# Who reads with a stride: rows written in plain order by VectorE, and transposes on TensorE that read every 8th or 4th column

## What is computed

```python
def rms_norm(x, g):
    y = x * lax.rsqrt(jnp.mean(x * x, axis=-1, keepdims=True) + EPS)
    return y * g
...
    # every token takes 2 of 32 experts; tokens are sorted by expert into blocks of 128
    def expert_block(args):
        xblk, e = args                       # 128 tokens x 1024
        hid = jax.nn.silu(xblk @ w_gate[e]) * (xblk @ w_up[e])     # 128 x 512
        return hid @ w_down[e]               # 128 x 1024
...
    x = x + hierarchical_moe(rms_norm(x, norm_ffn_g), ...)
```

## Time and profile before

| | |
|---|---|
| median of 3 runs | 2146.08 us (2141.89 to 2154.14) |
| the profiled execution | 2152.06 us, span of its trace 2150.2 us |
| TensorE busy | 2092.8 us, 97% |
| VectorE busy | 1303.7 us, 61% |
| ScalarE busy | 1073.8 us, 50% |
| mean DMA rate | 184 GB/s, up to 395 GB/s in the slices of the expert stage |

### The profile page before, as it was taken

The page is one execution under the profiler, slowest core; times in us unless marked ns, Lnnn a source line. Parts: engine busy times, 40 slices in busy tenths (PEclk is TensorE's granted clock), DMA queues, the critical chain, the costliest instruction groups (busy, mean ns, idle before and its releaser), DMA issues.

```text
span 2150.2 us, 30216 instructions
## 1 busy us (share of the span) xinstructions
PE 2092.8 (97%) x10268; PEld 1730.2 (80%) x10268; DVE 1303.7 (61%) x1645; ACT 1073.8 (50%) x1582; POOL 511.6 (24%) x653
## 2 busy tenths in 40 slices
PE   8999999999999999999999999989999999999997
PEld 7788888888788888897888888757788788878886
DVE  5654233465555233555643434458899999899994
ACT  4453333343442332344523232137787788778884
POOL 4251011220541011213500012113212234332221
PEclk9999999999999999999999999999999999999999
DMA  7213222433213323452122225579999998997973
GB/s 229 92 40 98 88 87 92 173 130 108 74 40 108 98 79 98 163 171 69 40 85 82 81 96 205 206 271 357 386 395 394 394 340 299 392 384 262 325 260 88
DMA packets 108657, 396.72 MB, mean 184 GB/s; under 512 B 9282, under 2 KB 15603, under 8 KB 82964
## 3 DMA queue, kind: packets, MB, share of 16 engines
q1 hardware_dynamic: 91812, 335.64, 42.0%
q0 software_dynamic: 16752, 59.83, 10.5%
HBM read 402.78 MB, written 34.60 MB: 203 GB/s over the span
## 4 chain that ended last, share of the span: by engine, by line
PE 42%; DMA 10%; DVE 2%; issue 2%; ACT 2%; SPq 0%; POOL 0%; POOLq 0%; ACTq 0%; DVEq 0%
DMA held_wu<-w_up_e 5%; PE main L512 3%; PE main L514 3%; PE main L513 3%; DMA y<-e_yo,e_prv 2%; PE main L500 2%; PE main L502 2%; PE main L501 2%; PE main L1988 2%; PE main L1990 2%; PE main L1989 2%; DMA e_xg<-h2s,e_nxt 2%; PE main L1976 2%; PE main L1975 2%; PE main L1974 2%
## 5 line engine op out<-in xcount | busy, mean ns | idle before, releaser
L959 DVE TENSOR_TENSOR w_lo<-raw,w_hi 128x1024 fp32r<-128x1024 f32 (+1 forms) x216 | 250.3, 1180 | 320.3 <-ACT w_hi L705 320.2
L705 ACT ACTIVATE w_hi<-raw 128x1024 fp32r<-128x1024 f32 (+1 forms) x216 | 211.7, 1006 | 141.9 <-PE main L514 73.9
L512 PE MATMUL main<-e_g_hi,w_hi 128*128 128x512 f32 x576 | 237.6, 413 | 0.0
L514 PE MATMUL main<-e_g_hi,w_lo 128*128 128x512 f32 x576 | 226.1, 392 | 0.0
L513 PE MATMUL main<-e_g_lo,w_hi 128*128 128x512 f32 x576 | 225.4, 391 | 0.0
L500 PE MATMUL main<-w_hi,e_g_hi 128*128 128x512 f32 (+1 forms) x560 | 203.6, 364 | 2.3 <-DVE e_g_lo L973 2.3
L502 PE MATMUL main<-w_hi,e_g_lo 128*128 128x512 f32 (+1 forms) x560 | 200.2, 357 | 0.0
L501 PE MATMUL main<-w_lo,e_g_hi 128*128 128x512 f32 (+1 forms) x560 | 200.0, 357 | 0.0
L2097 DVE TENSOR_TENSOR e_d_lo<-held_wd,e_d_hi 128x2048 fp32r<-128x2048 f32 x76 | 173.1, 2288 | 36.2 <-ACT e_d_hi L2034 36.1
L2097 DVE TENSOR_TENSOR e_u_lo<-held_wu,e_u_hi 128x2048 fp32r<-128x2048 f32 x76 | 173.7, 2285 | 25.6 <-ACT e_u_hi L2034 25.6
L2097 DVE TENSOR_TENSOR e_g_lo<-held_wg,e_g_hi 128x2048 fp32r<-128x2048 f32 x76 | 173.5, 2283 | 2.5 <-ACT e_g_hi L2034 2.4
(11 more groups left out here) (349 smaller groups left out, 4786.5 us busy)
## 6 DMA issues: line engine op xcount, KB each, us to landing
held_wg<-w_gate_e SPq DMA_DIRECT2D x78, 1024.0 KB
held_wu<-w_up_e SPq DMA_DIRECT2D x78, 1024.0 KB
held_wd<-w_down_e SPq DMA_DIRECT2D x76, 1024.0 KB
raw<-w_in SPq DMA_DIRECT2D x120, 512.0 KB, 3.6
raw<-w_proj_b SPq DMA_DIRECT2D x24, 512.0 KB, 3.6
raw<-w_proj_a SPq DMA_DIRECT2D x24, 512.0 KB, 3.6
raw<-w_out SPq DMA_DIRECT2D x24, 512.0 KB, 4.2
raw<-w_in SPq DMA_DIRECT2D x24, 256.0 KB, 4.6
```

What stands on the lines that cost most here:

```text
L512: pe.matmul(bank[:], hi[:, k, :], mov_hi[:, k, :], start=(k == 0), stop=False)
L514: mm = pe.matmul(bank[:], lo[:, k, :], mov_hi[:, k, :], start=False, stop=(k == KT - 1))
L705: act.activation(hi, buf, ACT.Copy).then_inc(w_hi_done, 1)
L959: dve.tensor_tensor(lo, buf, hi.bitcast(F32), ALU.subtract).then_inc(w_split, 1)
```

## The change

A helper `every(rows, n, k)` gives the view of every n-th column from column k on. VectorE's two instructions (three places in the code) lose their rearranged views and read and write in plain order. All transposes of `h2`, `xg` and `hid` take `every(...)` where they took 128 adjacent columns. `h2s` thus holds rows in natural order, and the turned tiles `h2T`, `xT` and `hidT` hold exactly what they held. The instructions, their number, their engines and their order are the same in both kernels.

```diff
+def every(rows, n, k):
+
+    return rows.rearrange("p (q k) -> p k q", k=n)[:, k, :]
...
                 for k in range(4):
-                    c = (4 * b + k) * P
-                    mm = pe.transpose(bank[:, k * P:(k + 1) * P], rows[:, c:c + P], ident)
+                    mm = pe.transpose(bank[:, k * P:(k + 1) * P], every(rows, KT, 4 * b + k), ident)
...
-            dve.scalar_tensor_tensor(out=rows.rearrange("p (k q) -> p k q", q=P),
-                                     in0=x2[:, t, :].rearrange("p (q k) -> p k q", q=P),
-                                     scalar=rsf[:, t:t + 1],
-                                     in1=gf_row.rearrange("p (q k) -> p k q", q=P),
-                                     op0=ALU.mult, op1=ALU.mult).then_inc(h2_ready, 1)
+            dve.scalar_tensor_tensor(out=rows, in0=x2[:, t, :], scalar=rsf[:, t:t + 1], in1=gf_row, op0=ALU.mult, op1=ALU.mult).then_inc(h2_ready, 1)
...
                 for k in range(4):
-                    c = (4 * b + k) * P
-                    mm = pe.transpose(ps_x[b][:, k * P:(k + 1) * P], xg[:, c:c + P], ident)
+                    mm = pe.transpose(ps_x[b][:, k * P:(k + 1) * P], every(xg, KT, 4 * b + k), ident)
...
             for k in range(DE // P):
-                mm = pe.transpose(ps_h[:, k * P:(k + 1) * P], hid[:, k * P:(k + 1) * P], ident)
+                mm = pe.transpose(ps_h[:, k * P:(k + 1) * P], every(hid, DE // P, k), ident)
...
-            dve.scalar_tensor_tensor(out=hid.rearrange("p (k q) -> p k q", q=P),
-                                     in0=th.rearrange("p (q k) -> p k q", q=P), scalar=0.5,
-                                     in1=ps_u[:].rearrange("p (q k) -> p k q", q=P),
-                                     op0=ALU.mult, op1=ALU.mult).then_inc(hid_done, 1)
+            dve.scalar_tensor_tensor(out=hid, in0=th, scalar=0.5, in1=ps_u[:], op0=ALU.mult, op1=ALU.mult).then_inc(hid_done, 1)
```

More of the change, by code:

```diff
@@ L1630, in turn_x @@
             for k in range(4):
-                c = (4 * b + k) * P
-                mm = pe.transpose(bank[:, k * P:(k + 1) * P], xg[:, c:c + P], ident)
+                mm = pe.transpose(bank[:, k * P:(k + 1) * P], every(xg, KT, 4 * b + k), ident)
             mm.then_inc(s_x_ps, 1)
@@ L1660, in turn_hidden @@
         for k in range(DE // P):
-            mm = pe.transpose(bank[:, k * P:(k + 1) * P], hid[:, k * P:(k + 1) * P], ident)
+            mm = pe.transpose(bank[:, k * P:(k + 1) * P], every(hid, DE // P, k), ident)
         mm.then_inc(s_h_ps, 1)
@@ L1712, in glu @@
             dve.wait_ge(s_h_ps, s)
-        dve.scalar_tensor_tensor(out=hid.rearrange("p (k q) -> p k q", q=P), in0=th[s].rearrange("p (q k) -> p k q", q=P), scalar=0.5,
-                                 in1=main[2 * s + 1][:].rearrange("p (q k) -> p k q", q=P), op0=ALU.mult,
-                                 op1=ALU.mult).then_inc(s_hid_done, 1)
+        dve.scalar_tensor_tensor(out=hid, in0=th[s], scalar=0.5, in1=main[2 * s + 1][:], op0=ALU.mult, op1=ALU.mult).then_inc(s_hid_done, 1)
     held["chosen_dve"] = {"glu": glu}
```

## The result

The changed kernel takes 2139.24 us (median of 14 runs, 2135.10 to 2143.47); beside it, on the same chip, the kernel before took 2149.48 us (14 runs, 2141.69 to 2161.65). The ratio is 0.9949 [0.9933, 0.9966]: about 11 us or 0.5% faster. Predicted was 2185.2, 1.8% slower. The sign was wrong.

A forecast was written before the change was run, and what follows sets the result against it. The prediction took TensorE, 97% busy, as the bound, with DMA-bound stretches among the expert blocks. Its slower transposes added 41.1 us, less VectorE's 2.0: +39.1 on the median 2146.08 gave 2185.2 us, 1.8% slower, range 2140 to 2212.

The forecast's parts named there:

- the pricing of TensorE's load: TensorE's stepped transposes: each exposed load costs 0.113 us more eight apart, 0.100 four apart, taken from VectorE's rows; 1.09 a block.
- if it gets longer, the row gets longer by as much: TensorE's rows of transposes: the load is exposed, so extra load time lengthens the row, except for a row's first load.
- the 41.1 us of the sum: TensorE's added transpose time over expert blocks, last block, chosen blocks and turns of h, before subtracting VectorE's 2.0 us.
- The reading that the load is what spaces the transposes: TensorE's transposes: 0.109 us apart where the identity's stream would need 0.057, so the weight load sets the spacing.
- The first rival: TensorE's load does not care how its columns lie; only 2.0 us gained, 2144, no measurable change; chance 19%.
- the four places on the chain: Chain of waits: VectorE's rewritten instructions count only at h_last and three times at e_hid, 2.0 us gained.
- one long wait for a gather: Expert intervals from 1833.00 to 1928.40 us: the wait absorbs TensorE's extra time, adding between 0 and 5.4, taken as +1.5.
- h_last (0.8 forecast): Rewritten VectorE instruction on the chain of waits, there at 2.09 us: the cheaper norm gains 0.8 us.
- The second rival: Expert blocks: the shorter glu starts weight loads earlier, shrinking TensorE's 19.7 us of waiting; 2124 at best; chance 3%.
- the loop of weight loads: DMA-bound expert blocks: chain circles through weight load (13.88), ScalarE's rounding (1.93) and VectorE's remainder (2.30).
- The third: TensorE's stepped load takes three times the plain one (+0.218 us); about 2236 us; chance 5%.
- VectorE's own prices: VectorE's plain instructions: norm_f 2181 to 1280 ns, glu's second half 1079 to 680 ns; 26.8 us less work.

The follow-up runs named there:

- t9: Kernel before, with the turn of xg done four times over in each expert block (32 transposes, 128 adjacent columns each): 2228.95 us, one run.
- t10: Changed kernel, with the turn of xg done four times over in each expert block (32 transposes, every 8th column): 2228.77 us, one run.
- e3: Kernel before, with only TensorE's transposes of xg and hid in expert and chosen blocks stepping through columns, VectorE unchanged: 2151.0 us, ratio 1.0016.
- e4: Kernel before, with only VectorE made plain; transposes still read 128 adjacent columns, router's weights loaded to fit: 2140.1 us, ratio 0.9955.
- c6: Changed kernel plus an unused VectorE addition of 256 columns (about 0.42 us) behind each block's glu: 2139.88 us, ratio 0.9952 to before.
- e12: Kernel before with plain norm_f and stepped turns of h2 and xg, plus a 64-column VectorE reduction between up's and down's remainders: 2141.67 us, ratio 0.9971.
- e16: Second run of e12's code, the 64-column reduction between the remainders of up and down: 2141.76 us, ratio 0.9974 to before.
- e17: As e16, but with the 64-column reduction behind the glu instead of between the remainders: 2152.51 us, ratio 1.0033 to before.
- norm half: Kernel before, with only norm_f written plain and turns of h2 and xg reading every 8th column: 2146.41 us (0.9990), again 2143.17 us (0.9988).
- glu half: Kernel before, with only hid (the glu's second half) written plain and its turns reading every 4th column: 2143.69 us, ratio 0.9985.
- c7: Changed kernel plus an unused VectorE addition of 640 columns (about 0.8 us) behind each block's glu: 2151.18 us, ratio 0.9999 to before.

## Why the prediction was wrong

*The step that failed* is the pricing of TensorE's load: "For the upper one the nearest rows are VectorE's [...] I take the upper value." With the sentence before it, "if it gets longer, the row gets longer by as much", it gave the 41.1 us of the sum. A load that reads eight apart costs 0.003 us, not 0.113 (t9 against t10), 1/40 of it; a whole block, with its four loads four apart, pays 0.04 us and not 1.09. With that size the term is about 2 us. Two engines that read the same memory with the same steps do not pay alike. The reading that the load is what spaces the transposes was not refuted; but the text took a longer load for a longer spacing, and the 52 ns that it did get longer overlap with the next load. The earlier trace rows could have warned of this: before the change a load lasts 145 ns while the transposes are 109 ns apart, and 304 of them, 44 us in sum, keep PEld busy for only 36.6.

*The first rival* ("the load does not care") had the mechanism, at 19%, but its time, 2144, lay 5 us above the result. It rested on the other step that failed, "what counts are the four places on the chain", 2.0 us. The rest of the profile showed where else: VectorE's h stands ahead of e_g_lo at a group's end, and the waits of before charge 3.0 us to it between 430 and 910 us:

```profile
PE aux L450 <- DVE e_g_lo L973: 3.0, 2, 1.7
```

In the changed kernel this is 0.6. The prediction looked for the rewritten instruction as a releaser and not for what is queued behind it. It also saw "one long wait for a gather" in 1833 to 1928, and used it as a cushion for TensorE's extra time without asking what made the gather late. The ledger of the 14.0 us between the two profiles is: 2.5 at the groups' ends, 1.0 for h_last (0.8 forecast), 6.1 in the blocks, of which 4.8 are waits for gathers and 0.3 waits for hid, and 1.8 in the tail. The other 2.6 are not shown to be the change's: 0.7 that was there by 19 us, 3.1 for the clock of before at the seam, less 1.4 for that of the changed kernel at 1003 us, and 0.2 in small steps. So the size of the gain, about 11 us by the medians, is only in part traced to instructions.

*The second rival* ("the shorter glu opens the loop of weight loads", 3%) had the sign and the wrong place. The loop did not open: the stretch that it rules took 119.70 us for 119.60, with 13.3 us of idle for 13.5. The third, a load that pays threefold, is excluded.

*VectorE's own prices* were right: 1277 ns for 1280, 682 for 680, 25.4 us less work for 26.8.

*Memory lines.* The Trainium skill's page Advanced Engine Details and Errata, section SBUF Cachelines, was cited as the rule that speaks against the change. Here TensorE's load agrees with it in its duration (141 to 193 ns) and not in its throughput (3 ns of 109); VectorE's rows agree with it (0.88 and 0.78 ns an element). The load rule on the page TensorE: Matmul & The Clock Gate, section LDWEIGHTS (loading the stationary operand), with no word on the step, is the one that the 0.112 us between stepped transposes agrees with.

**Shown and argued.** Shown by runs: the load's price (e3 and e4, and by a row and the intervals of t9 and t10); that VectorE alone brings the gain (e4); that it is no matter of VectorE's total work (c6); that an opening between the remainders gains and the same work elsewhere loses (e12, e16, e17). Shown by rows of all profiles: that GpSimd's issue stands still while VectorE makes a remainder, and that the opening ends it; and that the norm half acts ahead of the blocks and the glu half in them. Only argued: that the opening gains time because it ends these issues, since TensorE's waits for gathers explain only a part of e17's loss. Not shown: that the wait for h_last lowers the clock. Still open: how the 4 to 5 us of the glu half divide between late gathers and a hid that is 0.4 us earlier. By their means the halves gain 3.4 and 4.8 us against the kernel before, 8.2 together, where both in one gain 9.6 to 11.5; the intervals, 2 to 4 us each, allow that they simply add. Why c7 loses all when c6 loses nothing was not followed up. None of these versions beats the changed kernel by more than the measurement tells.

## What to carry to other kernels

Where a layout must be undone by reading in steps, and TensorE turns the data anyway, let its transpose do it: its load of 128 fp32 columns costs 0.003 us more eight words apart and about 0.01 four apart, while VectorE pays 0.8 to 0.9 ns for every element in its row. Price an operation by the spacing of its neighbours or by many of them in a row, never by its duration nor by another engine's rows. And for an instruction that gets shorter, follow what stands behind it on its engine, through the list of waits, before counting it as hidden. Two profiles differ by more than the change: before a difference is laid to a cause, see in the other profiles whether it comes with that cause.

## What the runs showed of the hardware

- An issue of a gather by GpSimd, 0.99 us alone, took 2.1 to 7.6 us whenever it began inside one of VectorE's remainders with two inputs in SBUF (74 of 74 issues in 20 profiles), and ended about 0.95 us after VectorE started its next instruction or one of those behind it. Beginning elsewhere it took 1.35 us at most (696 issues). A reduction of 0.21 us between the remainders gave the norm half back 3.2 +/- 2.1 us.
- A weight load that reads 128 fp32 columns eight words apart lasts 192 ns instead of 145, and the transposes behind it come 0.003 us further apart.
- At the seam TensorE's granted clock fell to 1.2 GHz for some microseconds in six of 20 profiles, three of four with a wait of 0.8 to 0.9 us ahead of it and three of 16 without. It cost 1.7 to 3.4 us.
- The same expert weights in smaller packets (170097 for 108657 in all) cost about 20 us against e4 (2160.2 for 2140.1), and the intervals that wait for them took 19.6 us.
